# The norm's roots copied a tile earlier, and the forget gate's transposes moved behind the first tile of compressed keys

## The reference

```
h = rms_norm(x, g_attn)
z = h @ w_in
fq, fk, fv, f_logit, nq, kc, vc, ksl, vsl, kwn, vwn, n_gate, g_a, g_b = split(z)
log_f = log_sigmoid(f_logit + b_f);  c = cumsum(log_f)          # forgetting attention
fox  = softmax(fq fk^T * SCALE + c_q - c_k, causal) @ fv
kc', vc' = silu(blocks(kc or vc) @ w1) @ w2                     # compressed keys, values
nsa  = gates(n_gate) of [compressed, selected, windowed attention of nq]
```

## Time and profile before

| | us |
|---|---|
| median of 3 runs | 1610.99 (1609.95 to 1611.53) |
| profiled execution | 1608.34 |
| its span | 1606.5 |
| TensorE busy | 1534.5 (96%) |
| VectorE busy | 821.0 (51%) |
| ScalarE busy | 617.6 (38%) |
| GpSimd busy | 355.4 (22%) |

### The profile page before, as it was taken

How to read it: one execution, slowest core, us unless ns; L and a number is a source line. 1 busy time by engine, 2 the same in 40 slices (tenths; PEclk the granted TensorE clock), 3 DMA queues, 4 the chain that set the end, 5 groups by cost and what they waited for, 6 DMA issues and landing times.

```text
span 1606.5 us, 19519 instructions
## 1 busy us (share of the span) xinstructions
PE 1534.5 (96%) x7198; PEld 1219.5 (76%) x7202; DVE 821.0 (51%) x1644; ACT 617.6 (38%) x1118; POOL 355.4 (22%) x364
## 2 busy tenths in 40 slices
PE   6899989999999999999999999989999999999995
PEld 5687655688877888888888788856687888888884
DVE  6537566444444343343446697577364543443444
ACT  5423467422244222232346333556443322222222
POOL 3200345300020000000036524445441210220112
PEclk9999999999999999999999999999999999999998
DMA  5743300332233233323332653311422232332321
GB/s 193 131 108 95 103 1 14 112 98 93 91 92 92 92 92 96 101 92 104 93 98 68 155 148 119 112 47 56 155 90 81 92 105 93 95 102 92 101 79 56
DMA packets 46669, 154.11 MB, mean 96 GB/s; under 512 B 5698, under 2 KB 5890, under 8 KB 46576
## 3 DMA queue, kind: packets, MB, share of 16 engines
q1 hardware_dynamic: 41840, 137.63, 27.0%
q0 software_dynamic: 4736, 15.25, 4.6%
HBM read 142.78 MB, written 9.55 MB: 95 GB/s over the span
## 4 chain that ended last, share of the span: by engine, by line
PE 85%; DVE 8%; ACT 3%; issue 2%; DMA 1%; DVEq 0%; POOL 0%; SPq 0%; another core or an unknown queue 0%; ACTq 0%
PE PSA L578 83%; PE PSA L780 1%; DVE WL L1691 1%; DVE AR L1781 1%; ACT AR L1298 1%; DVE AR L1779 1%; PE PSA L924 1%; DMA WR<-w_in 1%; DVE AR L1806 0%; DVE AHL L1897 0%; ACT AHL L1346 0%; ACT WH L1226 0%; DVE AR L2274 0%; DVE AR L2367 0%; DMA AR<-AR 0%
## 5 line engine op out<-in xcount | busy, mean ns | idle before, releaser
L578 PE MATMUL PSA<-Ah,WH 128*128 128x512 f32 x1072 | 425.6, 397 | 18.7 <-DVE WL L1691 18.3
L578 PE MATMUL PSA<-Ah,WL 128*128 128x512 f32 x1072 | 420.7, 392 | 0.0
L578 PE MATMUL PSA<-Al,WH 128*128 128x512 f32 x1072 | 420.6, 392 | 0.0
L1226 ACT CAST WH<-WR 128x1024 fp32r<-128x1024 f32 (+3 forms) x234 | 240.8, 1031 | 227.7 <-PE PSA L578 222.6
L1691 DVE TENSOR_TENSOR WL<-WR,WH 128x1024 fp32r<-128x1024 f32 (+3 forms) x207 | 251.5, 1216 | 73.1 <-ACT WH L1226 72.6
L578 PEld LDWEIGHTS PSA<-Ah,WH 128*128 128x128 f32 x1072 | 203.5, 190 | 65.1 <-issue 22.3
L578 PEld LDWEIGHTS PSA<-Al,WH 128*128 128x128 f32 x1072 | 203.4, 190 | 42.9 <-issue 0.7
L578 PE MATMUL PSA<-Bh,WH 128*128 128x512 f32 (+1 forms) x592 | 230.6, 390 | 5.4 <-DVE Bl L1968 4.0
L578 PEld LDWEIGHTS PSA<-Ah,WL 128*128 128x128 f32 x1072 | 203.1, 189 | 42.8
L578 PE MATMUL PSA<-Bh,WL 128*128 128x512 f32 (+1 forms) x592 | 229.2, 387 | 0.0
L578 PE MATMUL PSA<-Bl,WH 128*128 128x512 f32 (+1 forms) x584 | 226.7, 388 | 0.0
(11 more groups left out here) (363 smaller groups left out, 1934.7 us busy)
## 6 DMA issues: line engine op xcount, KB each, us to landing
WR<-w_in SPq DMA_DIRECT2D x228, 512.0 KB, 3.5
gt_tmp<-AR SPq DMA_DIRECT2D x16, 256.0 KB, 2.2
WR<-w_in SPq DMA_DIRECT2D x8, 384.0 KB, 3.1
XT<-scr_tmp POOLq DMA_DIRECT2D x8, 264.0 KB, 12.1
XT<-xT_in SPq DMA_DIRECT2D x4, 512.0 KB, 8.2
XT<-scr_tmp POOLq DMA_DIRECT2D x8, 256.0 KB, 15.9
XT<-xT_in POOLq DMA_DIRECT2D x1, 2048.0 KB, 9.9
x_tmp<-XT POOLq DMA_DIRECT2D x1, 2048.0 KB, 7.6
```

The lines of the kernel that those rows point to most:

```text
L578: return pe.matmul(o, l, r, start=start, stop=stop)
L1226: ac.copy(WH[p][:, 0:n], WR[j % RAW][:, 0:n]).then_inc(w_hi, 1)
```

## The change

The diff does four things.

- VectorE copies the columns of roots behind the third fk tile instead of the fourth.
- TensorE transposes `FX` behind the matmuls of kv0 instead of ahead of them.
- ScalarE splits kv2 (the high half) ahead of the gate's first operation instead of behind the output gates' tanh.
- VectorE splits kv2 (the low half) ahead of the gate's bias instead of behind the gate.

```diff
@@ tensor_program
             tokmajor(tid["a2", 0], (3, 3, 2), 288, 0)
-
-            pe.wait_ge(g_dv.sem, g_dv.at("fx", 4))
-            for a in range(4):
-                last = pe.transpose(bank(4)[0:104, 128 * a:128 * a + 128], FX[:, a, :], ident)
-            last.then_inc(g_tr, 1)
             pe.wait_ge(e_a.sem, e_a.end("fv"))
             for i, b in enumerate((5, 6, 7, 0)):
                 feat(tid["kv", i], hA, 8, bank(b))
+                if i == 0:
+
+                    pe.wait_ge(g_dv.sem, g_dv.at("fx", 4))
+                    for a in range(4):
+                        last = pe.transpose(bank(4)[0:104, 128 * a:128 * a + 128], FX[:, a, :], ident)
+                    last.then_inc(g_tr, 1)
@@ scalar_program
             for i in range(3):
                 split_to(tid["a2", i] + 2)
+            split_to(tid["kv", 2])
 
             ac.wait_ge(g_dv.sem, g_dv.at("lf", 1))
@@ vector_program, loop over fk
-            dv.wait_ge(n_rc, 1)
-            dv.tensor_copy(RC[1], bank(7)[:, 0:4]).then_inc(n_rd, 1)
+                if i == 2:
+                    dv.wait_ge(n_rc, 1)
+                    dv.tensor_copy(RC[1], bank(7)[:, 0:4]).then_inc(n_rd, 1)
```

## The result

The changed kernel takes 1602.05 us (median of 4 runs, 1601.68 to 1603.95) against 1611.26 (median of 4, 1609.95 to 1614.39) for the kernel before on the same chip: ratio 0.9943, 95% interval 0.9923 to 0.9963. Its profiled execution took 1603.95 us with a span of 1602.1. The forecast was 1602.6.

What follows compares the result with a forecast made beforehand. TensorE's two stalls held 13.5 us, with VectorE's serial chain late next. The chain's 7.1 us plus 1.3 us of DMA relief gave 8.4 us, so 1602.6 us was forecast from a median of 1610.99; range 1599.6 to 1606.3.

Steps and rivals of the forecast that it cites:

- (a): Roots' copy behind the third fk tile: fv starts without a wait at full clock; fv and a2 end 7.5 us earlier.
- D: Time from the end of fk on TensorE to nq3's first matmul; 87.2 us before the change.
- (b): Transposes behind the first kv tile: their wait for VectorE goes wholly; the gate's bias starts 6.0 us earlier.
- (c): kv2's split ahead of the gate: free there, takes about 1.1 us off VectorE's chain; first edge copy 7.1 us earlier.
- The new stall: At kv3, TensorE waits for VectorE's low half, which is 3.0 us late.
- slow tail: Slow clock behind the wait at kv3: the tile takes 7.7 us, against 5.44 at full clock.
- (d): VectorE's wait for the DMAs that shift the compressed keys shrinks by 1.3 us, taken between 0 and 2.6.
- The sum: nq3 starts at 143.1 instead of 151.53, a gain of 8.4 us, passed on whole to the end.
- the other five signs: fv without wait; transposes near 104; bias near 105; wait near 116, then slow clock; shorter wait for shifted keys.
- R1: All of TensorE's time at both stalls comes back, 13.5 us plus 0.4 at nq3: 1597.1 us; chance 0.06.
- R2: Clock stays low longer at kv3, which takes 10.2 instead of 7.7 us; gain 6.2 us, 1604.8; chance 0.08.
- R3: kv2's weights land late and delay the gate: some 4 us slower, 1615, chance 0.03; gain under 3.2 us, 0.04.

## Why the prediction was right, point by point

- **(a) the roots.** fv starts at fk's end and fv and a2 take the forecast 34.5 us (67.80 to 102.28, the end of kv0 at 107.72 less a tile). 7.5 us forecast, 7.5 found. The experiment with this part alone shows that it carries nearly the whole gain: D falls by 7.4 of 7.9 us.
- **(b) the transposes.** The wait is gone and the bias comes 6.0 us earlier, as worked out. But these 6.0 us are (a)'s 7.5 less 1.5 that the transposes' move costs the chain: with the roots alone the bias comes 39.0 us after fk's end, with the whole change 40.6. The prediction said that the chain wins less than TensorE does; it didn't say how little is left of this part. With the splits but without (a) it gives 0.1 us in D. Next to (a) and (c) D is 1.2 higher with it than without it, since it delays a chain that is due at nq3 as early as TensorE is.
- **(c) the splits.** kv2's half runs right behind the copies into `FX`, free. Without it the whole change has 3.7 us more of D. The splits without the other two parts were not run.
- **The new stall.** 3.0 us at kv3 forecast, 3.01 found. Its slow tail was taken too long: 2.3 us forecast, 7 slow matmuls and some 1.5 us found. It didn't matter, because nq2 and nq3 wait for the chain anyway.
- **(d) the relief of the DMAs.** 1.3 us taken out of 0 to 2.6; found 0.8. This is the term that was mis-sized. With it D was forecast at 87.2 - 8.4 = 78.8 and is 79.3. Half of the two loads was gone, but not half of the delay. With no load beside the DMAs the relief is 2.6, as the bound said (3.66 us between the edge columns instead of 6.25).
- **The sum.** 8.4 us forecast, 7.9 in D; the medians of three comparisons differ by 9.2, 7.5 and 10.2 us, each with an interval of some 3 us on either side. On the clock of the profile before, nq3 starts at 143.6, forecast was 143.1; the other five signs came as listed. That the forecast of 1602.6 lies within 0.6 us of the median 1602.05 is in part luck: D fell 0.5 us short of its sum, and the changed kernel's median was 1604.18 and 1601.91 on the two other chips.
- **R1** is out: the whole of TensorE's 13.5 us doesn't come back. **R2** is out: the slow clock was shorter, not longer (kv3 took 7.0 us, R2 has 10.2). **R3**: its premise of a worst landing of 15.8 us was too low. A weight load took 17.3 us from issue to landing, a2's second tile was cast only at 87.21 because of it, and kv2's load was issued at 89.3 instead of the 86.5 that the forecast means on this clock:

```profile
87.21 0.92 ACT L1227 CAST WH<-WR 128x864 fp32r<-128x864 f32 x1 [7.36 <-DMA WR<-w_in]
```

  TensorE wanted that tile at about 94.3 (67.80, four fv tiles of 5.44 and 4.75 for a2's first tile, three eighths of its 12.7), 5 us after its low half was done at 89.2 (88.16 and 1.06 on VectorE), so nothing was lost. The prediction has no term for slower loads once (a) lets TensorE go on; yet in the twelve profiles with the roots' copy moved the longest weight load issued between 60 and 95 us takes 17.2 to 19.9 us, in the two without it 15.8 and 14.7. TensorE waited for none of them.

## What to carry to other kernels

Before a stall of the busiest engine is removed, work out when each engine behind it is due; the gain is the smallest of their leads, not the stall. An edit that lets the busy engine go on by delaying the start of another engine's serial chain can give back all that it wins: here removing 3.3 us of idling ahead of the transposes brought nothing, until the chain had been shortened (D 78.1 with the wait, 75.3 without it). Once the chain is the bound, look for its own waits (for the gate's logarithm, for a DMA) and put the independent pieces there.

## What was not expected of the hardware

- Executions of the same instructions up to fk differ by up to 3.6 us in when fk ends: 64.34 to 67.96 over the profiles here, and 67.80, 67.40 and 65.34 for three profiles of one and the same kernel. So one profile tells such kernels apart only by distances within the trace.
- After the same idle time of 3.30 us the slow clock lasted 11 matmuls in the kernel before, 5 and 8 in two profiles of the one with roots and splits; after 3.01 us it was 7. After 1.97 us of idling (at nq0, with kv3's split early) the first two matmuls came 0.31 us apart and the others 0.23, so the clock hadn't fallen. The Trainium skill ("TensorE: Matmul & The Clock Gate", section "Part 1: The HAM clock gate (the "warmup" mystery)") says of the slow matmuls at the start of a kernel that their number differs from run to run. These traces show the same for stalls in the middle of a kernel.
- The load of a2's second tile (432 KB) took 17.3 us from issue to landing beside the Toeplitz loads (`XT<-scr_tmp` in the earlier trace rows), where a weight load of 512 KB with less beside it took 3.8.
